# Hybrid GLA/SSD layer on one core: the SSD's within-chunk product in two column halves of 64 tokens

## What is computed

```
L = SSD_CHUNK                                  # 128 tokens
a_cum = cumsum(dt * A, over the chunk)
decay_ij = exp(where(causal, a_cum_i - a_cum_j, -inf))
cb = einsum('bcign,bcjgn->bcijg', Cm, Bm)
w = cb[..., None] * decay_ij * dt[:, :, None]
y = einsum('bcijgh,bcjghp->bcighp', w, x)      # <- the product in question
states = einsum('bcjgn,bcjghp->bcghpn', Bm, (decay_end * dt)[..., None] * x)
...                                            # scan over chunks
y = y + einsum('bcign,bcghpn,bcigh->bcighp', Cm, S_prev, exp(a_cum))
```

## Time and profile before

| | us |
|---|---|
| median of 3 runs | 1815.12 |
| lowest, highest | 1813.05, 1816.71 |
| the profiled execution | 1816.05 |
| its span in the trace | 1814.3 |

### The profile page before, as it was taken

One profiled execution on the slowest core, in us unless ns is written; L12 is line 12 of the kernel. 1 busy time (PEld: TensorE's weight loads), 2 busy tenths in 40 slices (PEclk: granted clock), 3 DMA queues, 4 the chain that ended last, 5 costly groups with the idle time before them and its releaser, 6 DMA issues. The chain is left out here.

```text
span 1814.3 us, 26153 instructions
## 1 busy us (share of the span) xinstructions
PE 1687.6 (93%) x9622; PEld 1458.2 (80%) x9622; DVE 878.4 (48%) x1603; ACT 784.7 (43%) x1390; POOL 242.7 (13%) x369
## 2 busy tenths in 40 slices
PE   3689899999999999979999999999999599999998
PEld 3478788887888888869989888889888377888886
DVE  5344444453433443447666668766776442222221
ACT  4454555445544554544555455555444441111110
POOL 5000100010000001001222222222222101000000
PEclk8799999999999999989999999999999799999999
DMA  9322151235122322223112134112110263222221
GB/s 278 127 88 87 60 169 59 72 109 163 61 79 78 110 64 66 82 86 101 64 66 93 64 104 134 65 65 94 64 52 35 93 241 118 92 92 92 92 95 44
DMA packets 105342, 172.20 MB, mean 95 GB/s; under 512 B 7587, under 2 KB 75443, under 8 KB 102310
## 3 DMA queue, kind: packets, MB, share of 16 engines
q1 hardware_dynamic: 102118, 154.05, 26.5%
q10 hardware_dynamic: 2304, 16.78, 2.5%
q0 software_dynamic: 832, 0.22, 0.2%
HBM read 137.21 MB, written 33.82 MB: 94 GB/s over the span
## 5 line engine op out<-in xcount | busy, mean ns | idle before, releaser
L1026 PE MATMUL ps<-hl,w 128*128 128x512 f32 x1488 | 376.7, 402 | 0.1
L1909 PE MATMUL ps<-d_w,d_yh 128*128 128x512 f32 x1536 | 354.2, 393 | 17.5 <-DVE d_yh L1866 10.9
L1909 PEld LDWEIGHTS ps<-d_w,d_yh 128*128 128x128 f32 x1536 | 290.3, 189 | 81.4 <-DVE d_yh L1866 11.3
L1026 PEld LDWEIGHTS ps<-hl,w 128*128 128x128 f32 x1488 | 275.9, 189 | 58.4 <-issue 1.4
L1645 PE MATMUL ps<-hl,w 128*128 128x256 f32 x2304 | 295.4, 288 | 4.3 <-PEq L258 4.3
L1645 PEld LDWEIGHTS ps<-hl,w 128*128 128x128 f32 x2304 | 283.3, 194 | 12.4 <-issue 12.4
L1032 PE MATMUL ps<-w,hl 128*128 128x256 f32 x1536 | 205.3, 291 | 2.0 <-DVE w L738 2.0
L1032 PEld LDWEIGHTS ps<-w,hl 128*128 128x128 f32 x1536 | 195.4, 195 | 4.9 <-DVE w L738 2.4
L1527 DVE SCALAR_TENSOR_TENSOR c_acc<-c_before,conv_col,c_acc 128x256 f32<-128x256 f32 x288 | 142.1, 494 | 78.4 <-ACT c_acc L1411 71.5
L1649 PE MATMUL ps<-hl 128*128 128x512 f32 x768 | 178.7, 392 | 0.0
L1649 PEld LDWEIGHTS ps<-hl 128*128 128x128 f32 x768 | 143.0, 188 | 29.4
(11 more groups left out here) (227 smaller groups left out, 2195.2 us busy)
## 6 DMA issues: line engine op xcount, KB each, us to landing
x_sb<-h SPq DMA_DIRECT2D x52, 512.0 KB, 3.9
c_ac<-step_sums ACTq DMA_DIRECT2D x16, 1024.0 KB, 4.7
w_raw<-in_w_in SPq DMA_DIRECT2D x30, 512.0 KB, 5.2
c_h_raw<-h SPq DMA_DIRECT2D x56, 256.0 KB, 2.8
d_y_raw<-mixed_in SPq DMA_DIRECT2D x7, 2048.0 KB, 9.0
ada<-in_ada_w SPq DMA_DIRECT2D x16, 512.0 KB, 11.4
x_sb<-in_x SPq DMA_DIRECT2D x16, 512.0 KB, 7.4
mixed_in<-y SPq DMA_DIRECT2D x32, 256.0 KB, 2.5
```

The lines of the kernel that those rows point to most:

```text
L1026: mm = pe.matmul(ps[:, PROJ + u % 2, :], w[:, u, k, a, :], hl[:, par, k, b, :], start=(k == 0 and i == 0), stop=(k == KT - 1 and i == 2))
L1909: mm = pe.matmul(ps[:, 2 * t + j, :], yh[:, t, f, a, :], w[:, f, c, j * 512:(j + 1) * 512], start=(f == 0 and i == 0), stop=(f == FT - 1 a ...
```

## The change

Each matmul of L1678 becomes two. The first takes target tokens 0 to 63 of the chunk as its 64 stationary columns and writes partitions 0 to 63 of bank Y; the second takes tokens 64 to 127 and writes partitions 64 to 127. An output on partitions 0 to 63 or 64 to 127 goes with the lower or the upper half of the array's columns. Both read all 128 partitions of the same `xdt[:, h, :]`. The order is head by head, lower half and then upper half. The last matmul of the tile still raises `y_done`. What is read, multiplied and written is the same, and no wait, no other engine's program and no DMA is changed.

```
     PROJ, X, BC, Y, YI, ST, YT = 0, 2, 3, 4, 5, 6, 7
+    CH = P // 2
     QS = 4
...
                     for h in range(HG):
-                        mm = pe.matmul(ps[:, Y, h * SP_:(h + 1) * SP_], decay[:, h, t * P:(t + 1) * P], xdt[:, h, :], start=True, stop=True)
+                        for i in range(2):
+                            mm = pe.matmul(ps[i * CH:(i + 1) * CH, Y, h * SP_:(h + 1) * SP_],
+                                           decay[:, h, t * P + i * CH:t * P + (i + 1) * CH], xdt[:, h, :], start=True,
+                                           stop=True)
                     mm.then_inc(y_done, 1)
```

## The result

The changed kernel takes 1801.82 us (median of five, 1801.02 to 1804.36), the kernel before, measured again beside it, 1816.62. The ratio is 0.992, 95% interval 0.991 to 0.993: 0.8% faster, 14 to 15 us. When the changed kernel was measured again, at the end of the experiments, one of its six executions was slow (9376 us): it counts in the median given there and not in the ratio. I had forecast 11 us slower. The first rival, the two halves side by side, was priced at 17.4 us faster, and that is what happened, a little smaller.

The account below looks back on a forecast made before the run. TensorE bounds the SSD stage and weight loads bound L1678; inside +0.10, entry +0.145, exit +0.14 make 0.385 us a tile, 12.3 us for 32 tiles, less 1 for waits: +11 us on 1816.05, 1827; range 1796 to 1850.

Parts of the forecast that it names:

- The first rival: L1678: half loads for both array halves run side by side; tile 0.55 us shorter, 17.4 us faster, 1797.7; chance 0.27.
- What bounds the kernel: SSD stage: TensorE without gaps in 29 of 32 tiles, L1678 bound by weight loads, 0.108 of 0.111 us a pair.
- Inside the 32 pairs: L1678: narrow loads come one after another, 0.0575 us a pair, 31 distances instead of 15; +0.10 us a tile.
- both bounds: Inside L1678's pairs: 0.84 us less if the halves never met, 1.77 more without gain from the narrower load.
- Entering and leaving the narrow form: Around L1678: 0.09 us switch each side plus an uncovered load; entry +0.145, exit +0.14 us a tile.
- half the overlap: Side-by-side case at L1678 with only half of the overlap: -0.13 us a tile, 4 us, 1811.
- The floor: L1678: short pairs cannot go below about 0.08 us; 35 us slower, 1850, or 1881 at 0.111; chance 0.13.
- No overlap of loads and matmuls in the narrow form: L1678: a narrow pair takes load, stream and 0.09 us in turn; 148 us slower, 1963; chance 0.03.
- No switch: L1678: the 64-column form is not cut off from its neighbours; only 3 us slower, 1818.3; chance 0.08.
- the break-even: L1678: side by side wins once the overlap saves more than 0.285 us of the 1.67 inside a tile.

Follow-up runs that it names:

- the run on one half: Changed kernel with all 32 narrow matmuls of a tile writing partitions 0 to 63, upper half left out; 1827.78 us, ratio 1.006 to the kernel before.
- the alternating run: Changed kernel with heads 0, 2, 4, 6 in halves and heads 1, 3, 5, 7 full width; 1841.0 us, ratio 1.013 to the kernel before.
- quarters: Changed kernel with each head in four pieces of 32 target tokens instead of two halves; 1798.49 us, ratio 0.990 to the kernel before.

## Why the prediction was wrong, point by point

**What bounds the kernel** was right. TensorE without gaps, the line bound by its loads, three of 32 tiles in a wait: the 0.51 us taken from a tile came out of the whole time in 29 of them, and the waits grew only a little. In the changed kernel, TensorE's waits for VectorE ahead of the line:

```profile
PE ps L1680 <- DVE c_btok L1557: 8.0, 3, 3.7
```

It is 8.0 us instead of the 7.4 of the earlier trace rows; the waits for ScalarE at the turn grew from 5.4 to 6.7.

**Inside the 32 pairs** is the step that failed: +0.10 us forecast, -0.80 measured. Before, 15 distances of 0.111 lay between first and last matmul, 1.67 us (1.89 less the 0.219 that a matmul lasts when it does not wait for its load); after, the 32 matmuls start within 1.15 - 0.222 = 0.93, less the uncovered first load (0.054, which the sum has in the entry) 0.87. The price of one narrow pair was right (0.0575 against 0.058 on one half). Wrong was the reading "one load ahead, in order, gives a row of loads, whatever half of the array they are for". In every row of before the next load shares columns with the one ahead of it, as in the run on one half, where loads come one by one too. That only one was ahead there says nothing of a load for other columns. I took a limit of the place for a limit of the queue. The rows could not decide it; both bounds that I wrote down (0.84 less, 1.77 more) were open, and the value near the middle had no row behind it. Nor does a load always begin with the matmul ahead of it, as I had read: in the single records of the tile a load begins 0.056 us after the start of the matmul ahead (923.872 and 923.816), and with it only where that matmul's own load was done.

**Entering and leaving the narrow form** was right in kind and size. The stream of L1673's second matmul ends at 959.49 + 0.43 = 959.92 and the first narrow load is at 960.01: 0.09 us, as at L1098. On the other side the state matmul lasts 0.70 instead of 0.65: its load is uncovered. A pair of switches cost 0.29 in the alternating run, 0.285 in the sum. The Trainium skill's rule on draining ("TensorEngine Tiling (Array Packing)", "Key Properties") holds, by those 0.09 us on each side. The other sentence of that section, on tiles that load and multiply in parallel, holds too, and it is where the trace and my reading parted.

**The rivals.** Side by side, at 0.27: it happened, with 14 to 15 us instead of 17.4, since a tile gave 0.51 instead of 0.55 (the inside 0.80 instead of 0.83), and since I multiplied by 32 where 29 tiles count. Its case of half the overlap (1811) did not come, because the other half starts past a waiting second pass. The floor: none at 0.028 us a pair, nor at 0.014 with quarters. No overlap of loads and matmuls in the narrow form: no; loads lie under matmuls on either half, also when all are on one. That is against the rule on row groups in the Trainium skill, "TensorE: Matmul & The Clock Gate", section "The mechanism", as far as this kernel goes. No switch: refuted by the 0.09.

**The range and the chances.** 1801.8 lies in the range of 1796 to 1850, which reached down for this case; the likeliest case and the 0.65 on slower were on the wrong side. With the switches known and the inside unknown, the break-even was an overlap of 0.285 of 1.67 us; a little over a third of the possible overlap would have won. I should have given that margin more weight than a pattern seen only where it could not be otherwise.

## What to carry to other kernels

Where float32 matmuls with few moving columns (64 here; no other type was run) are bound by their weight loads, split the stationary operand by columns and send the pieces to different output partitions, alternating from piece to piece; the pieces load and stream at the same time. Keep the narrow form in one block, since each pair of switches costs about 0.29 us here, so that three or four 128-column float32 matmuls (0.107 us gained each, the first of the line half of it) are needed to pay for it; four of them gained 0.08 us a tile. And when a trace shows that something never happens, ask first whether it could have happened there.

## What the runs showed of the hardware that I had not expected

Pieces that write different output partitions, and so use different columns of the array, load their weights at the same time (a tile's 32 matmuls in 1.15 us, 2.08 when all use one half), four at a time with quarters (64 in 1.10). TensorE starts a piece for another part past two or three waiting pairs, not past more: with sixteen, eight, four and two pairs in a row for one half a tile's product takes 1.68, 1.32, 0.98 and 0.93 us from first to last start. And streams of 512 columns on two halves overlap too: four matmuls in 1.08 us, where two of full width take 1.02.
